# Who splits the first 64 key tiles, and one-hot arrays by fours of tokens

## The chip, the cores and the metric

The kernel runs on one core of a Trainium2 chip. The time is the device time of one launch in microseconds (us). TensorE is PE (its weight loads are PEld), VectorE is DVE, ScalarE is ACT, GpSimd is POOL, and SyncE is SP, which here only issues DMAs.

## The reference, cut to what matters

One decoder block on 256 tokens of width 1024: a mixer (conformer convolution and dilated attention), and then a layer of 16384 one-neuron experts, of which each token picks 16 in each of 8 heads:

```python
q = (xc @ w_q).reshape(TOKEN_CHUNK, PEER_HEADS, 2, half)
s = einsum('thpd,hpnd->thpn', q, sub_keys)            # 128 scores for each of 16 half keys
top_s, top_i = lax.top_k(s, PEER_TOPK)
cand = top_s[:, :, 0, :, None] + top_s[:, :, 1, None, :]
best_s, best_c = lax.top_k(cand.reshape(...), PEER_TOPK)
e = i1 * PEER_N_KEYS + i2                             # from top_i at best_c
gate = softmax(best_s)
h = einsum('thkd,td->thk', u_tab[e], xc)
act = gelu(h) * gate
y = einsum('thk,thkd->td', act, v_tab[e])
```

The kernel does not gather. It computes the gelu of all 16384 products with `u_tab`, multiplies each by its gate (zero for an expert that was not picked), and multiplies by all of `v_tab`.

## The kernel before, in words

All weights come in tiles of 128 x 1024 float32 (512 KB): 76 tiles `front` of the mixer and of `w_q`, 128 tiles of `u_tab` and 128 tiles of `v_tab`. They pass through one ring of four slots (RING). A tile in slot s goes through four engines:

- SP loads `raw[s]` when the lower part of the tile that held the slot before has been written (`load`, L348 to L351).
- ACT writes `hi[s]`, the tile rounded to the matmul's fast float32 format, once PE is done with the tile before in that slot (`split_hi`, L303 to L310).
- DVE or POOL writes `lo[s] = raw - hi` (`split_lo`, L319 to L324). `by_dve` (L312 to L314) says which of the two: DVE takes slot 3, and from tile G_SHARED = 143 on slot 1 too. Each of the two engines works through its instructions in the order in which they are written, so a split waits for what is written ahead of it.
- PE multiplies hi by hi, hi by the vector's low part and lo by hi: 24 matmuls of 256 columns a `u` tile (L1055), 12 of 512 columns a `v` tile (L1326).

ACT splits three tiles ahead of PE (LEAD = 3): while PE computes tile n, ACT writes `hi` of tile n + 3, and then the gelu of tile n (L573).

The expert layer has four stages. The first runs over the first 64 `u` tiles. In it, DVE works through 43 steps of the top-16 selection (`top_step`, L890; steps 0 to 15 are the first top 16, step 16 converts the indices, then for each of two chunks of 128 tokens one step that forms the candidates, L871, four of the second top 16, L857 to L862, one of small operations, L907 to L910, six that look the picked indices up, L881, L886 and L888 twice, and a last one, L916). A table `tile_of` spreads these steps over 48 of the 64 tiles, but only through the order of writing: nothing but the splits that stand among them (L934 to L941, one in four tiles) holds DVE back. Near the end PE transposes the picked indices and gates (L1297, L1301).

The second stage runs over the other 64 `u` tiles, the third over the first 64 `v` tiles. In both, every second tile, the gates of 8 tokens (TOK) are spread over 64 second keys: DVE makes `eqB` (L965), `ohA` (L967) and `ohB` (L971), float16 arrays of ones and zeros or gates, PE multiplies them token by token (L1283, 16 matmuls of 64 columns), and DVE multiplies the result into the gelu values (L983). In the third stage DVE also writes the low part of each vector, `nrm_lo` (L990). The fourth stage runs over the last 64 `v` tiles. The first u tiles up to tile 78 of all are split outside the stages' loops, by the same rule. POOL fills `iota_nk` (L409) between tile 78 and tile 79, the tile with which its loop over the 64 tiles of the change begins.

The one-hot arrays hold the tokens by pairs: in `ohA[:, g, q // PAIR, :, q % PAIR]` the 128 values of one token lie two elements (4 bytes) apart, and the two tokens of a pair alternate.

Of the kernel before, what the change touches and what calls it, by code (L numbers as in the profile page):

```python
# [10 lines left out]
F16 = mybir.dt.float16  # L11
ALU = mybir.AluOpType
# [3 lines left out]
P = 128  # L16
D = 1024
T = 256
# [10 lines left out]
PH, NK, TOPK = 8, 128, 16  # L29
# [14 lines left out]
LEAD = 3  # L44
# [6 lines left out]
WARM_UP = 12  # L51
G_SHARED = N_FRONT + HALF + LEAD
TOK = 8
PAIR = 2
GROUPS_N = T // TOK


# [79 lines left out]
    FREED[_job] = _n[freed_by_dve(_job)]  # L137


PAIRS = [(0, 2), (1, 3), (4, 6), (5, 7), (8, 10), (9, 11)]  # L140


C_N1, C_N2, C_GLU, C_DW, C_DWB = 0, 8, 16, 24, 24 + CB * TAPS
# [8 lines left out]
def hybrid_block(nc, x_t, front, cols, rel_bias, onehot, sub_keys, u_tiles, v_tiles, out):  # L152
    toeplitz = nc.dram_tensor("toeplitz", (HEADS, P * BW), F32, kind="Internal").ap()
    with ExitStack() as ctx:
        def sb(name, shape, dt=F32, stack=ctx):
            return stack.enter_context(nc.sbuf_tensor(name, shape, dt))
# [46 lines left out]
        resid = tmp("resid", [P, KB, T])  # L203
        inner.close()
        act = sb("act", [P, NK, T])
        iota_nk = sb("iota_nk", [P, NK, PAIR], F16)
        keys = sb("keys", [P, 2, T], F16)

        parts = sb("parts", [P, T // PAIR, 2, PAIR], F16)
        ohA = sb("ohA", [P, 2, TOK // PAIR, NK, PAIR], F16)  # L210
        eqB = sb("eqB", [P, 2, TOK // PAIR, HALF, PAIR], F16)
        ohB = sb("ohB", [P, 2, TOK // PAIR, 2, HALF, PAIR], F16)

        p3 = prob[:, :].rearrange("p (h n) -> p h n", n=BW)
        qT = prob[:, 0:HALVES * T].rearrange("p (u t) -> p u t", t=T)
# [79 lines left out]
        def slot_of(base, j):  # L295
            return (base + j) % RING
# [14 lines left out]

        def by_dve(base, j):  # L312

            return slot_of(base, j) == 3 or (base + j >= G_SHARED and slot_of(base, j) == 1)  # L314

        def wait_lo(eng, base, it, j):
# [65 lines left out]
        @block.gpsimd  # L382
        def _(pool):

            pool.memset(relx[BUCKETS:BUCKETS + 1, :], NEG).then_inc(const, 1)
            pool.wait_ge(const, 1)
            pool.memset(ones[:, :], 1.0).then_inc(const, 1)
            pool.memset(ident[:, :], 0.0).then_inc(const, 1)
            pool.memset(u_pad[:, :, 0:TAPS - 1], 0.0).then_inc(const, 1)
            pool.memset(kmask[:, :], 0.0).then_inc(const, 1)  # L390
            pool.wait_ge(const, 5)
            for r in range(2):
                pool.memset(kmask[r * HD:(r + 1) * HD, HEADS - 2 + r:HEADS - 1 + r], 1.0).then_inc(const, 1)
                pool.wait_ge(const, 6 + r)
            pool.affine_select(out=ident[:, :], in_=ident[:, :], compare_op=ALU.not_equal, fill=1.0,
                               base=0, pattern=[[-1, P]], channel_multiplier=1).then_inc(const, 1)
            pool.iota(iota[:, :], pattern=[[1, TOPK]], base=0, channel_multiplier=0,
                      allow_small_or_imprecise_dtypes=True).then_inc(const, 1)

            def lo_of(g):  # L400
                if not by_dve(g, 0):
                    split_lo(pool, g, 0, 0)

            for g in range(N_FRONT + LEAD):
                lo_of(g)

            pool.wait_ge(y_began, 1)
            pool.wait_ge(normed, 2 * KB)
            pool.iota(iota_nk[:, :, :], pattern=[[1, NK], [0, PAIR]], base=0, channel_multiplier=0,  # L409
                      allow_small_or_imprecise_dtypes=True).then_inc(const, 1)  # L410
            for base, tiles in ((U0 + LEAD, HALF), (G_SHARED, N_U + N_V - RING - HALF)):
                with pool.Fori(0, tiles // RING) as it:
                    for j in range(RING):
                        if not by_dve(base, j):
                            split_lo(pool, base, it, j)

        @block.scalar
        def _(a):
# [25 lines left out]
            split_hi(a, 2, 0, 0)  # L444

            def exp_of(s):
                c, pair = divmod(s, len(PAIRS))
                w = P * (c + 1)
                a.wait_ge(score_max, s + 1)
                for h in PAIRS[pair]:  # L450
                    pr = p3[:, h, c * P:c * P + w]
                    col = c * HEADS + h
                    a.activation(pr, pr, ACT.Exp, bias=negm[:, col:col + 1],
                                 accum_out=lsum[:, col:col + 1]).then_inc(exps, 1)
# [166 lines left out]
        def _(dve):  # L621
# [78 lines left out]

            def score(s):

                c, pair = divmod(s, len(PAIRS))
                h0 = PAIRS[pair][0]
                w = P * (c + 1)
                job_done(dve, ("score", s))
                for r, h in enumerate(PAIRS[pair]):
                    col = c * HEADS + h
                    ins = dve.scalar_tensor_tensor(out=p3[:, h, c * P:c * P + w],
                                                   in0=bank[BANK_OF[("score", s)]][:, r * w:(r + 1) * w],  # L710
                                                   scalar=rq[:, col:col + 1], in1=bias[:, h, T - w:T],
                                                   op0=ALU.mult, op1=ALU.add)
                    ins.then_inc(dve_evac if r else biased, 1)
                freed(dve, ("score", s))
                dve.wait_ge(biased, s + 1)
                dve.tensor_reduce(negm[:, c * HEADS + h0:c * HEADS + h0 + 3:2], p3[:, h0:h0 + 3:2, c * P:c * P + w],
                                  AX.X, ALU.max, negate=True).then_inc(score_max, 1)
# [214 lines left out]
            weights = [21] * HALVES + [10] + TC * ([23] + [35] * (PH // 2) + [8] + [23] * 6 + [3])  # L932
            tile_of = [int(TOP_TILES * sum(weights[:n]) / sum(weights)) for n in range(len(weights))]
            for i in range(HALF):  # L934
                if by_dve(U0 + LEAD, i):
                    split_lo(dve, U0 + LEAD, 0, i)
                for n, tile in enumerate(tile_of):
                    if tile == i:
                        top_step(n)
                if i == EXP_TILE + 2:  # L940
                    softmax_gates()  # L941
# [1 line left out]
            dve.tensor_copy(keys[:, :, :], bank[6][:, :].rearrange("p (a t) -> p a t", a=2)).then_inc(pick_ready, 1)  # L943
            dve.wait_ge(pick_T, 2)
            link(dve.tensor_scalar(pickf[:, 0, :], bank[7][:, 0:T], GATE_SCALE, None, ALU.mult))
            picked = pickf[:, 0, :].rearrange("p (a b) -> p a b", b=PAIR)
            link(dve.tensor_copy(parts[:, :, 0, :], picked))
            dve.tensor_tensor(parts[:, :, 1, :], picked, parts[:, :, 0, :], ALU.subtract).then_inc(pick_ready, 1)
            dve.wait_ge(pick_ready, 2)
# [2 lines left out]
            def one_hots(half, it, g):  # L952

                n = it * 2 + (half * GROUPS_N + g)
                t = bass.ds(it * (2 * TOK) + g * TOK, TOK)

                wait(dve, gate_mm, n - 1)

                def at(x, m):
                    return x.rearrange("p (a b) -> p a b", b=PAIR).unsqueeze(2).broadcast_to([P, TOK // PAIR, m, PAIR])  # L960

                def every_pair(x, m):
                    return x.unsqueeze(1).broadcast_to([P, TOK // PAIR, m, PAIR])

                dve.tensor_tensor(eqB[:, g % 2], every_pair(iota_nk[:, half * HALF:(half + 1) * HALF, :], HALF),  # L965
                                  at(keys[:, 1, t], HALF), ALU.is_equal).then_inc(second, 1)
                dve.tensor_tensor(ohA[:, g % 2], every_pair(iota_nk[:, :, :], NK), at(keys[:, 0, t], NK),  # L967
                                  ALU.is_equal).then_inc(spread, 1)
                dve.wait_ge(second, n + 1)
                two = bass.ds(it * (2 * TOK // PAIR) + g * (TOK // PAIR), TOK // PAIR)  # L970
                dve.tensor_tensor(  # L971
                    ohB[:, g % 2].rearrange("p a i n b -> p (a i) n b"),
                    eqB[:, g % 2].unsqueeze(2).broadcast_to([P, TOK // PAIR, 2, HALF, PAIR]),
                    parts[:, two, :, :].rearrange("p a i b -> p (a i) b").unsqueeze(2)
                    .broadcast_to([P, 2 * TOK // PAIR, HALF, PAIR]), ALU.mult).then_inc(spread, 1)

            def multiply(half, it, g):

# [56 lines left out]
        def _(pe):  # L1035
# [104 lines left out]
                step(ins)  # L1140

            def scores(s):
                c, pair = divmod(s, len(PAIRS))
                w = P * (c + 1)
                b = start(("score", s))
                freed(pe, ("kb", AB // 2 - 1))
                for r, h in enumerate(PAIRS[pair]):
                    rows = slice((h % 2) * HD, (h % 2 + 1) * HD)
                    ins = pe.matmul(b[:, r * w:(r + 1) * w], qk[rows, h // 2, c * P:(c + 1) * P],  # L1149
                                    qk[rows, AB + h // 2, 0:w], start=r == 0, stop=True, skip_group_check=True)  # L1150
                step(ins)
# [125 lines left out]
            def gates(half, it, g):  # L1277

                n = it * 2 + (half * GROUPS_N + g)
                pe.wait_ge(spread, n * 2 + 2)  # L1280
                for q in range(TOK):
                    for i in range(2):
                        ins = pe.matmul(bank[6 + g][:, q * HALF:(q + 1) * HALF], ohA[:, g, q // PAIR, :, q % PAIR],  # L1283
                                        ohB[:, g, q // PAIR, i, :, q % PAIR], start=i == 0, stop=i == 1, skip_group_check=True)
                ins.then_inc(gate_mm, 1)

            for j in range(RING):
# [131 lines left out]
```

## Time and profile before

| | us |
|---|---|
| median of 3 runs | 1069.43 |
| lowest, highest | 1066.47, 1072.64 |
| the profiled execution | 1069.04 |
| its span (first to last instruction) | 1067.3 |
| PE, DVE, ACT, POOL busy | 1049.8, 751.4, 509.7, 514.0 |

The mean granted TensorE clock of the profiled execution is 0.988 of full speed. The chain that ended last is 91% PE. By the trace the stages of the expert layer are: first stage about 298 to 491 us, second to 694, third to 886, fourth to 1063. A busy PE says little by itself, since matmuls are pipelined; what counts is how far their starts are apart, and the gaps. The duration of a DVE or POOL instruction in these rows includes time in which it had been issued and was held up, with no semaphore in play.

### The profile page before, as it was taken

How to read it: one execution, taken by the hardware profiler on the slowest of the kernel's cores; microseconds unless marked ns; L12 is line 12 of the kernel's file. 1: busy time of each engine (PE TensorE's matmuls, PEld its weight loads, DVE VectorE, ACT ScalarE, POOL GpSimd, SP SyncE). 2: the span in 40 equal slices, each digit the busy share in tenths (PEclk: the TensorE clock that was granted, in tenths of full speed). 3: DMA queues.
4: the chain of work that ended last, by engine and by line, in shares of the span. 5: the costliest groups of instructions: out<-in, count | busy, mean ns of one | idle time of the engine just before them, and what ended most of it. 6: DMA issues, size and time to landing. Idle time of an engine off the chain costs nothing.

```text
span 1067.3 us, 21882 instructions
## 1 busy us (share of the span) xinstructions
PE 1049.8 (98%) x7850; PEld 961.8 (90%) x7850; DVE 751.4 (70%) x1232; ACT 509.7 (48%) x798; POOL 514.0 (48%) x216
## 2 busy tenths in 40 slices
PE   8999999999999998999999999999999999999998
PEld 6999898999999998999999999978887777888886
DVE  5375868744079899918555555599999997777775
ACT  5453667545454443454444444444444444444553
POOL 3654452654646694964344333444434434444442
PEclk8999999999999998999999999999999999999999
DMA  5864342644535544465554455545554555666662
GB/s 195 267 209 139 125 149 84 216 160 141 182 133 183 191 148 166 140 214 174 167 172 158 161 173 168 166 158 177 177 172 162 177 177 178 197 196 188 190 194 97
DMA packets 52258, 181.91 MB, mean 170 GB/s; under 512 B 5851, under 2 KB 9051, under 8 KB 52092
## 3 DMA queue, kind: packets, MB, share of 16 engines
q1 hardware_dynamic: 52220, 181.41, 52.0%
q8 instruction: 24, 0.39, 0.1%
q14 instruction: 14, 0.11, 0.0%
HBM read 177.97 MB, written 3.41 MB: 170 GB/s over the span
## 4 chain that ended last, share of the span: by engine, by line
PE 91%; DVE 7%; issue 1%; ACT 1%; DMA 0%; SPq 0%; ACTq 0%; DVEq 0%
PE bank L1055 49%; PE bank L1326 33%; PE bank L1283 3%; PE bank L1136 2%; DVE lo L323 1%; PE bank L1065 1%; PE bank L1149 1%; PE bank L1263 1%; DVE gsig L829 1%; DVE prob L748 1%; DMA relx<-rel_bias 0%; DVE act L881 0%; DVE act L886 0%; DVE act L871 0%; PE bank L1243 0%
## 5 line engine op out<-in xcount | busy, mean ns | idle before, releaser
L323 POOL TENSOR_TENSOR lo<-raw,hi 128x1024 fp32r<-128x1024 f32 x202 | 511.1, 2535 | 538.5 <-ACT hi L310 538.1
L310 ACT CAST hi<-raw 128x1024 fp32r<-128x1024 f32 x332 | 347.9, 1048 | 200.9 <-PE bank L1326 189.8
L1055 PE MATMUL bank<-nrm_hi,hi 128*128 128x256 f32 x1504 | 433.4, 288 | 7.5 <-DVE lo L323 5.1
L1055 PE MATMUL bank<-nrm_lo,hi 128*128 128x256 f32 x1504 | 428.1, 285 | 0.0
L1055 PE MATMUL bank<-nrm_hi,lo 128*128 128x256 f32 x1504 | 427.9, 285 | 0.0
L1055 PEld LDWEIGHTS bank<-nrm_hi,hi 128*128 128x128 f32 x1504 | 291.1, 194 | 12.9 <-issue 7.7
L1055 PEld LDWEIGHTS bank<-nrm_lo,hi 128*128 128x128 f32 x1504 | 291.4, 194 | 0.1
L1055 PEld LDWEIGHTS bank<-nrm_hi,lo 128*128 128x128 f32 x1504 | 291.1, 194 | 0.0
L323 DVE TENSOR_TENSOR lo<-raw,hi 128x1024 fp32r<-128x1024 f32 x130 | 173.6, 1336 | 111.0 <-ACT hi L310 110.5
L990 DVE TENSOR_TENSOR nrm_lo<-act,nrm_hi 128x256 fp32r<-128x256 f32 x128 | 151.0, 1182 | 51.2 <-ACT nrm_hi L598 51.1
L1326 PE MATMUL bank<-hi,nrm_hi 128*128 128x512 f32 x512 | 160.6, 395 | 0.7 <-ACT nrm_hi L598 0.7
L1326 PE MATMUL bank<-hi,nrm_lo 128*128 128x512 f32 x512 | 158.9, 391 | 0.3 <-DVE nrm_lo L990 0.3
L1326 PE MATMUL bank<-lo,nrm_hi 128*128 128x512 f32 x512 | 158.0, 390 | 0.0
L573 ACT ACTIVATE act<-bank 128x256 f32 x128 | 49.1, 384 | 218.0 <-PE bank L1055 217.9
L1326 PEld LDWEIGHTS bank<-hi,nrm_lo 128*128 128x128 f32 x512 | 95.1, 188 | 22.9 <-DVE nrm_lo L990 3.7
L1326 PEld LDWEIGHTS bank<-lo,nrm_hi 128*128 128x128 f32 x512 | 96.1, 188 | 20.2
L1326 PEld LDWEIGHTS bank<-hi,nrm_hi 128*128 128x128 f32 x512 | 93.7, 188 | 18.7 <-issue 0.8
L983 DVE SCALAR_TENSOR_TENSOR act<-bank,act 128x512 f32 (+1 forms) x64 | 43.9, 685 | 83.6 <-PE bank L1283 83.6
L971 DVE TENSOR_TENSOR ohB<-eqB,parts 128x1024 f16<-128x1024 f16 x64 | 59.2, 925 | 0.0
L967 DVE TENSOR_TENSOR ohA<-iota_nk,keys 128x1024 f16<-128x1024 f16 x64 | 52.5, 820 | 0.0
L598 ACT CAST nrm_hi<-act 128x256 fp32r (+1 forms) x128 | 51.2, 402 | 0.1
L689 DVE SCALAR_TENSOR_TENSOR bank<-u_pad,prm,bank 128x256 f32<-128x256 f32 x116 | 46.7, 481 | 0.0
(172 smaller groups left out, 764.8 us busy)
## 6 DMA issues: line engine op xcount, KB each, us to landing
raw<-u_tiles SPq DMA_DIRECT2D x128, 512.0 KB, 3.4
raw<-v_tiles SPq DMA_DIRECT2D x128, 512.0 KB, 3.4
raw<-front SPq DMA_DIRECT2D x76, 512.0 KB, 3.4
toeplitz<-prob SPq DMA_DIRECT2D x12, 192.0 KB, 4.4
bias<-toeplitz SPq DMA_DIRECT2D x12, 128.0 KB, 4.1
resid<-x_t SPq DMA_DIRECT2D x2, 512.0 KB, 4.5
qk<-sub_keys SPq DMA_DIRECT2D x1, 1024.0 KB, 6.8
y<-act SPq DMA_DIRECT2D x2, 512.0 KB, 2.6
```

The source lines that it names most:

```text
L310: act_e.copy(hi[:, s, :], raw[:, s, :]).then_inc(hi_ready, 1)
L323: eng.tensor_tensor(lo[:, s, :], raw[:, s, :], hi[:, s, :].bitcast(F32), ALU.subtract)\
L573: a.activation(act[:, it * 4 + (base_i + j), :], bank[4 + j % 2][:, 0:T], ACT.Gelu).then_inc(gelu_done, 1)
L598: a.copy(nrm_hi[:, (base_i + j) % RING, :], act[:, it * 4 + (base_i + j), :]).then_inc(a_hi, 1)
L689: dve.scalar_tensor_tensor(out=acc[:, b, :] if w == TAPS - 1 else part_sum, in0=src, scalar=wt, in1=part_sum, op0=ALU.mult, op1=ALU.add).t ...
L967: dve.tensor_tensor(ohA[:, g % 2], every_pair(iota_nk[:, :, :], NK), at(keys[:, 0, t], NK), ALU.is_equal).then_inc(spread, 1)
L971: dve.tensor_tensor(ohB[:, g % 2].rearrange("p a i n b -> p (a i) n b"), eqB[:, g % 2].unsqueeze(2).broadcast_to([P, TOK // PAIR, 2, HALF, ...
L983: dve.scalar_tensor_tensor(out=av, in0=gv, scalar=1.0 / GATE_SCALE, in1=av, op0=ALU.mult, op1=ALU.mult)\
L990: dve.tensor_tensor(nrm_lo[:, s, :], act[:, it * 4 + (base_i + j), :], nrm_hi[:, s, :].bitcast(F32), ALU.subtract).then_inc(a_lo, 1)
L1055: ins = pe.matmul(dst, w_[:, s, u * P:(u + 1) * P], x_[:, k, :], start=first and i == 0 and p_ == 0, stop=last and i == n - 1 and p_ == 2)
L1283: ins = pe.matmul(bank[6 + g][:, q * HALF:(q + 1) * HALF], ohA[:, g, q // PAIR, :, q % PAIR], ohB[:, g, q // PAIR, i, :, q % PAIR], start= ...
L1326: ins = pe.matmul(bank[2 * c + half][:, :], a_[:, j, c * P:(c + 1) * P], v_[:, j, half * 512:(half + 1) * 512], start=False, stop=stop and ...
```

## The change

- `by_dve` returns False for the tiles 79 to 142 (from U0 + LEAD up to G_SHARED), whatever their slot. POOL's loop over these 64 tiles then splits all of them in place of three in four, and the 16 splits that stood among DVE's top-16 steps are gone. All other tiles are split as before.
- PAIR = 2 becomes QUAD = 4 in the layout of `iota_nk`, `parts`, `ohA`, `eqB` and `ohB`: the values of one token lie four elements (8 bytes) apart, and four tokens alternate. The element counts of the DVE instructions, and all matmuls, stay the same; the runs of adjacent elements with one broadcast value, which had two elements, have four. `iota_nk` has 512 elements a partition in place of 256.
- The views through which DVE writes and reads these arrays (`picked`, `at`, `every_pair`, `two` and the operands of L971) have the same replacement. The list PAIRS of attention heads is only renamed.

```diff
-PAIR = 2
+QUAD = 4
-        iota_nk = sb("iota_nk", [P, NK, PAIR], F16)
+        iota_nk = sb("iota_nk", [P, NK, QUAD], F16)
-        parts = sb("parts", [P, T // PAIR, 2, PAIR], F16)
-        ohA = sb("ohA", [P, 2, TOK // PAIR, NK, PAIR], F16)
-        eqB = sb("eqB", [P, 2, TOK // PAIR, HALF, PAIR], F16)
-        ohB = sb("ohB", [P, 2, TOK // PAIR, 2, HALF, PAIR], F16)
+        parts = sb("parts", [P, T // QUAD, 2, QUAD], F16)
+        ohA = sb("ohA", [P, 2, TOK // QUAD, NK, QUAD], F16)
+        eqB = sb("eqB", [P, 2, TOK // QUAD, HALF, QUAD], F16)
+        ohB = sb("ohB", [P, 2, TOK // QUAD, 2, HALF, QUAD], F16)
...
         def by_dve(base, j):
 
+            if U0 + LEAD <= base + j < G_SHARED:
+                return False
             return slot_of(base, j) == 3 or (base + j >= G_SHARED and slot_of(base, j) == 1)
...
-            pool.iota(iota_nk[:, :, :], pattern=[[1, NK], [0, PAIR]], base=0, channel_multiplier=0,
+            pool.iota(iota_nk[:, :, :], pattern=[[1, NK], [0, QUAD]], base=0, channel_multiplier=0,
...
             for i in range(HALF):
-                if by_dve(U0 + LEAD, i):
-                    split_lo(dve, U0 + LEAD, 0, i)
                 for n, tile in enumerate(tile_of):
                     if tile == i:
                         top_step(n)
...
-                        ins = pe.matmul(bank[6 + g][:, q * HALF:(q + 1) * HALF], ohA[:, g, q // PAIR, :, q % PAIR],
-                                        ohB[:, g, q // PAIR, i, :, q % PAIR], start=i == 0, stop=i == 1, skip_group_check=True)
+                        ins = pe.matmul(bank[6 + g][:, q * HALF:(q + 1) * HALF], ohA[:, g, q // QUAD, :, q % QUAD],
+                                        ohB[:, g, q // QUAD, i, :, q % QUAD], start=i == 0, stop=i == 1, skip_group_check=True)
```

## Rows read from the trace of the kernel before

**Rows 1.** The page, part 1: busy us, share of the span, instructions.
```profile
PE 1049.8 (98%) x7850; PEld 961.8 (90%) x7850; DVE 751.4 (70%) x1232; ACT 509.7 (48%) x798; POOL 514.0 (48%) x216
```

**Rows 2.** What PE waited for: us in total, times, longest; the largest of nine.
```profile
PE bank L1055 <- DVE lo L323: 5.1, 1, 5.1
```

**Rows 3.** The chain of waits from 290 to 500 us: start, us, what.
```profile
290.65 7.14 PE bank L1263 x64
297.79 80.71 PE bank L1055 x672
...
412.40 2.73 DVE lo L323
...
490.81 0.50 PE bank L1283 x16
```

**Rows 4.** Timeline of ACT: start, us, instruction, count, idle before and its releaser.
```profile
407.43 0.38 ACT L573 ACTIVATE act<-bank 128x256 f32 x1 [1.56 <-PE bank L1055]
407.71 1.04 ACT L310 CAST hi<-raw 128x1024 fp32r<-128x1024 f32 x1
410.31 0.38 ACT L573 ACTIVATE act<-bank 128x256 f32 x1 [1.55 <-PE bank L1055]
...
420.86 0.38 ACT L573 ACTIVATE act<-bank 128x256 f32 x1 [9.24 <-PE bank L1055]
...
426.96 0.39 ACT L573 ACTIVATE act<-bank 128x256 f32 x1 [1.56 <-PE bank L1055]
```

**Rows 5.** Stretches: us, PE busy, granted PE clock, DMA share, GB/s.
```profile
410.00:415.00 5.00, 0.17 (x2) 0.96 0.00 0
415.00:420.00 5.00, 4.74 (x22) 0.50 0.62 215
```

**Rows 6.** Timeline of POOL in the first stage: splits, alone and beside DVE.
```profile
365.63 2.40 POOL L323 TENSOR_TENSOR lo<-raw,hi 128x1024 fp32r<-128x1024 f32 x1 [0.48 <-ACT hi L310]
371.38 4.02 POOL L323 TENSOR_TENSOR lo<-raw,hi 128x1024 fp32r<-128x1024 f32 x1 [3.36 <-ACT hi L310]
375.37 4.45 POOL L323 TENSOR_TENSOR lo<-raw,hi 128x1024 fp32r<-128x1024 f32 x1
...
408.83 2.38 POOL L323 TENSOR_TENSOR lo<-raw,hi 128x1024 fp32r<-128x1024 f32 x1 [0.47 <-ACT hi L310]
```

**Rows 7.** Timeline of DVE in the same stretch.
```profile
370.85 2.29 DVE L881 TENSOR_TENSOR act<-act,iota 128x2048 f32<-128x2048 f32 x1
373.17 4.38 DVE L886 TENSOR_TENSOR act<-act 128x2048 f32<-128x2048 f32 x1
377.59 2.29 DVE L888 TENSOR_REDUCE act<-act 128x128 f32<-128x2048 f32 x1
...
394.45 3.47 DVE L323 TENSOR_TENSOR lo<-raw,hi 128x1024 fp32r<-128x1024 f32 x1
...
400.37 4.38 DVE L871 TENSOR_TENSOR act<-act 128x2048 f32<-128x2048 f32 x1
```

**Rows 8.** Groups of DVE instructions, 500 to 690 us: busy, mean ns, idle before.
```profile
L323 DVE TENSOR_TENSOR lo<-raw,hi 128x1024 fp32r<-128x1024 f32 x30 | 36.8, 1225 | 6.5 <-ACT hi L310 6.2
...
L967 DVE TENSOR_TENSOR ohA<-iota_nk,keys 128x1024 f16<-128x1024 f16 x30 | 20.6, 685 | 0.0
...
L965 DVE TENSOR_TENSOR eqB<-iota_nk,keys 128x512 f16<-128x512 f16 x30 | 12.6, 419 | 0.0
```

**Rows 9.** Timeline of DVE late in the third stage.
```profile
850.51 2.63 DVE L990 TENSOR_TENSOR nrm_lo<-act,nrm_hi 128x256 fp32r<-128x256 f32 x1
...
856.67 2.61 DVE L990 TENSOR_TENSOR nrm_lo<-act,nrm_hi 128x256 fp32r<-128x256 f32 x1
```

**Rows 10.** The chain of waits in the third stage: start, us, what.
```profile
730.41 0.50 PE bank L1283 x16
730.91 5.55 PE bank L1326 x24
```

**Rows 11.** Line 409: POOL's iota, duration ns min/median/max, first and last start.
```profile
L409 POOL IOTA iota_nk<- x1: 1504/1504/1504, 291.5 to 291.5; 128x256 f16 x1
```

More of the change, by code:

```diff
@@ L137 @@
     FREED[_job] = _n[freed_by_dve(_job)]
-PAIRS = [(0, 2), (1, 3), (4, 6), (5, 7), (8, 10), (9, 11)]
+QUADS = [(0, 2), (1, 3), (4, 6), (5, 7), (8, 10), (9, 11)]
 C_N1, C_N2, C_GLU, C_DW, C_DWB = 0, 8, 16, 24, 24 + CB * TAPS
@@ L446, in exp_of @@
             def exp_of(s):
-                c, pair = divmod(s, len(PAIRS))
+                c, pair = divmod(s, len(QUADS))
                 w = P * (c + 1)
                 a.wait_ge(score_max, s + 1)
-                for h in PAIRS[pair]:
+                for h in QUADS[pair]:
                     pr = p3[:, h, c * P:c * P + w]
@@ L701, in score @@
             def score(s):
-                c, pair = divmod(s, len(PAIRS))
-                h0 = PAIRS[pair][0]
+                c, pair = divmod(s, len(QUADS))
+                h0 = QUADS[pair][0]
                 w = P * (c + 1)
                 job_done(dve, ("score", s))
-                for r, h in enumerate(PAIRS[pair]):
+                for r, h in enumerate(QUADS[pair]):
                     col = c * HEADS + h
@@ L945, in _ @@
             link(dve.tensor_scalar(pickf[:, 0, :], bank[7][:, 0:T], GATE_SCALE, None, ALU.mult))
-            picked = pickf[:, 0, :].rearrange("p (a b) -> p a b", b=PAIR)
+            picked = pickf[:, 0, :].rearrange("p (a b) -> p a b", b=QUAD)
             link(dve.tensor_copy(parts[:, :, 0, :], picked))
@@ L959, in at @@
                 def at(x, m):
-                    return x.rearrange("p (a b) -> p a b", b=PAIR).unsqueeze(2).broadcast_to([P, TOK // PAIR, m, PAIR])
+                    return x.rearrange("p (a b) -> p a b", b=QUAD).unsqueeze(2).broadcast_to([P, TOK // QUAD, m, QUAD])
                 def every_pair(x, m):
-                    return x.unsqueeze(1).broadcast_to([P, TOK // PAIR, m, PAIR])
+                    return x.unsqueeze(1).broadcast_to([P, TOK // QUAD, m, QUAD])
                 dve.tensor_tensor(eqB[:, g % 2], every_pair(iota_nk[:, half * HALF:(half + 1) * HALF, :], HALF),
@@ L969, in one_hots @@
                 dve.wait_ge(second, n + 1)
-                two = bass.ds(it * (2 * TOK // PAIR) + g * (TOK // PAIR), TOK // PAIR)
+                two = bass.ds(it * (2 * TOK // QUAD) + g * (TOK // QUAD), TOK // QUAD)
                 dve.tensor_tensor(
                     ohB[:, g % 2].rearrange("p a i n b -> p (a i) n b"),
-                    eqB[:, g % 2].unsqueeze(2).broadcast_to([P, TOK // PAIR, 2, HALF, PAIR]),
+                    eqB[:, g % 2].unsqueeze(2).broadcast_to([P, TOK // QUAD, 2, HALF, QUAD]),
                     parts[:, two, :, :].rearrange("p a i b -> p (a i) b").unsqueeze(2)
-                    .broadcast_to([P, 2 * TOK // PAIR, HALF, PAIR]), ALU.mult).then_inc(spread, 1)
+                    .broadcast_to([P, 2 * TOK // QUAD, HALF, QUAD]), ALU.mult).then_inc(spread, 1)
             def multiply(half, it, g):
@@ L1142, in scores @@
             def scores(s):
-                c, pair = divmod(s, len(PAIRS))
+                c, pair = divmod(s, len(QUADS))
                 w = P * (c + 1)
@@ L1146, in scores @@
                 freed(pe, ("kb", AB // 2 - 1))
-                for r, h in enumerate(PAIRS[pair]):
+                for r, h in enumerate(QUADS[pair]):
                     rows = slice((h % 2) * HD, (h % 2 + 1) * HD)
```

## The prediction

> **What bounds the kernel now.** I read the busy times first, then what PE waited for, then the chain of waits, and last the timelines around the one long gap. PE is busy 98% of the span and DVE 70% [rows 1], so only what changes PE's pace or its gaps moves the time. PE waits long for an operand once: 5.1 us for a low part from DVE [rows 2], which is `by_dve`'s slot 3 among the top-16 steps. Otherwise the first stage is dense: 672 matmuls in 80.71 us are 28 tiles at 2.88 us [rows 3]. The gap has a second part. After it PE runs at granted clock 0.50 for a while, 1.2 in place of 2.4 GHz [rows 5]. The gelus on ACT follow PE's tiles and count the whole loss: from 410.31 to 426.96 there are three tiles, 16.65 us in place of 3 x 2.88 = 8.64, so the episode costs 8.0 us [rows 4].
>
> **Why DVE was late.** ACT had this tile's `hi` by about 403.1 (one of the splits three tiles ahead, 1.04 us each [rows 4]), but DVE came to the split at 412.40 [rows 3], after a candidate step that began at 400.37 [rows 7] and two pairs of second top-16 steps up to 412.40, 7.6 us.
>
> **The change, part by part.** *DVE's 16 splits go.* Alone such a split takes 1.2 us [rows 8]. DVE then has no wait left among its steps and runs through them ahead of the tiles; it had time to spare in this stage apart from the one late split, so what it saves is worth nothing but the end of that episode: -8.0 us, if POOL is on time. What DVE does next (the gates' operands) waits for PE's transposes at tile 60 and is not earlier in a way that PE sees.
>
> *POOL gets 16 more.* Alone it needs 2.40 us a tile [rows 6] against PE's 2.88, so it now keeps up with every tile with 0.48 to spare. How far may it fall behind? ACT casts from 407.71, POOL splits from 408.83 for 2.38 and is done at 411.21; the tile is for PE three tiles after the one that began at about 407.4, at 407.4 + 8.64 = 416.0 [rows 4, 6]. So the reserve is 4.8 us. Before, a POOL that was behind got a free tile in four; now it catches up by 0.48 a tile only.
>
> What makes it fall behind is in the durations. From 371.38 POOL's splits take 4.02 and 4.45 us, and DVE's L886 takes 4.38 where L881, of the same size, took 2.29 [rows 6, 7]. The ends explain it: L881 ends at 373.14 and POOL's split at 375.40, 2.3 us later; L886 ends at 377.55, 2.2 us after that; POOL's next one at 379.82, 2.3 us after that. The two engines take turns: a POOL split and a DVE instruction with two large SBUF inputs do not run together. L888, a reduction with one input, takes 2.29 with a split beside it [rows 7], so it takes no turn. Each long turn of DVE costs POOL 4.45 - 2.40 = 2.05 us.
>
> Debt of POOL, first burst: the lookups of chunk 0 are four long turns (L881, L886, twice), L916 is a short one, and the candidates of chunk 1 (L871) a fifth long one. I charge 5 x 2.05 + 0.2 = 10.5 us. It lasts 5 x 4.38 + 2 x 2.29 + 2.5 = 29 us, 10.1 tiles, which give back 10.1 x 0.48 = 4.8. Net 5.6 against a reserve of 4.8: PE stands 0.8 us. Followed turn by turn, as PE starts a tile only on the whole split, it is about 1.4. Then the second top 16 of chunk 1, four pairs in 2 x 7.6 us and 1.05 of small operations, is 5.6 tiles, 2.7 us back, so 2.1 of debt is left. Second burst: four long turns and a short one, 8.4 us, over 24.6 us, 8.5 tiles, 4.1 back: 6.4, over the reserve by 1.6; turn by turn about 2.6. Together 2.4 by the sums and 4.0 by turns; I take 4.0, as single pauses of 0.5 to 1.5 us. With POOL's own part of a turn 0.05 us shorter or longer the turns give 2.7 or 5.1. The clock stays at 2.4 GHz in my forecast: it fell behind a pause of 5.1 us [rows 2, 5], and these are shorter. First stage: -8.0 + 4.0 = -4.0.
>
> The candidates of chunk 0 come alone, one turn, and are hidden by the reserve. SP loads the next tile of a slot after `lo` is written: a late split delays the load by as much, but the cast that it feeds is itself wanted only after PE is through with the tile. At the reserve's end this closes to about nothing, and I cost it at 0; uncovered it would add some tenths of a us at each of five pauses, 1 us in all. Removing the slot-3 split from DVE at the very end of the stage also puts four splits in a row on POOL while DVE makes its first one-hots, whose turns are short (0.4 to 0.7 us alone [rows 8]): inside the reserve.
>
> *The iota* doubles to 512 elements: 1.5 us [rows 11] becomes at most 3.0, in a hole of POOL before the first tile of its loop: its end moves from 293.0 to about 294.5, and the split behind it starts after 300 us, with the cast of tile 79 behind the end of the scores at 297.79 [rows 3]. 0.
>
> *Fours on DVE.* `eqB` has 512 elements and takes 0.419, `ohA` 1024 and takes 0.685: 0.52 ns an element. The float32 split takes 1.225 for 1024 and L881 2.29 for 2048: 1.04 ns an element [rows 7, 8]. So pairs already run at twice the float32 rate, the fastest of any two-input row here, with the rest a fixed part that no layout touches. I take 0. Bounds: a quarter of the one-hots' time gained or lost, (0.419 + 2 x 0.685) / 4 = 0.45 us a group. In the second stage DVE waits much of the time, so that is hidden. In the third it is not: DVE's period of two tiles is 856.67 - 850.51 = 6.16 us late in the stage [rows 9], against PE's own 6.05, two `v` tiles in 5.55 and the gates' 0.50 [rows 10]. A gain is worth no more than the 0.1 us a group, some 2 us in all; a loss counts in full, 32 x 0.45 = 14 us.
>
> The Trainium skill, "VectorE: DVE Perf Modes", section "The perf-mode tier table", says that a two-input instruction on 16-bit data reaches two elements a cycle and no more. The rows' factor of two agrees, and by it the layout by fours gains nothing.
>
> *Fours on PE.* 1024 matmuls (64 groups of 16) read weights and columns with an 8-byte step in place of 4. Now a group takes 0.50 us, 31 ns a matmul [rows 3]. No row has an 8-byte step. Lower bound: 256 columns take 80.71 / 672 = 120 ns [rows 3], so 64 take 30 at the same rate, and there is 1 ns a matmul to gain, 1 us in all. Upper bound, by the nearest matmuls with 128 weights that are loaded at the float32 rate: 7.14 us for 64, 112 ns each [rows 3], so 1024 x 0.081 = 83 us. If only the column read halves, 1024 x 0.031 = 32 us. I take 0, nearest to the row of the same instruction at half the step.
>
> The Trainium skill, "SBUF — State Buffer", section "Door 1: The DMA port swizzle", speaks of 16-byte lines, with full bandwidth as long as two accesses in a row hit one line. An 8-byte step is just inside that, and by it the cost is 0; no row here shows it.
>
> **Sum.** 1069.04 for the profiled execution (span 1067.3 and 1.7 around it) - 4.0 = 1065.0. That execution stands 0.4 under the median 1069.43, so against the median I say 1065.4.
>
> **Rivals.**
> (A) POOL keeps up: the turns cost less than charged (DVE, now early, meets POOL's idle time), PE never stands. Gain 8.0: 1061.4. For it: each lone contended split is absorbed today. Against: two splits in a row already took 8.4 us for 5.8 us of PE [rows 6].
> (B) The pauses pull the clock down: two or three of them, up to 1.5 us each with one tile between, bring a stretch at 1.2 GHz like that of rows 5, which cost 8.0 - 5.1 = 2.9 us. One or two such: 1068 to 1071. For it: the drop after the one gap. Against: in such a stretch PE wants tiles more slowly, and POOL catches up.
> (C) The other side: PE's gate matmuls slow down with the 8-byte step, in the second and third stage, where PE sets the pace. It decides from 4.0 / 1024 = 4 ns a matmul on. At 62 ns: 1065.4 + 32 = 1097. A small form (35 to 40 ns) gives 1070 to 1075. Against it: pairs already have a step and show 31 ns.
> (D) The late split is not always that late. At 394.45 POOL had started its split just ahead of DVE's, and DVE's took 3.47 [rows 7]; had DVE been first, the chain up to 412.40 would be 2.3 us shorter, the gap some 2.8 us and perhaps without the clock's fall. If the runs of before differ in this (1066.47 to 1072.64), the gain shows as less: 1067.
>
> **How the numbers follow.** Forecast 0.47 (1062.5 to 1067.5), A 0.18, B 0.10, C 0.13, D 0.12. The middle 8 in 10 runs from 1060 (most of A inside) to 1073 (C's large form left out, about 0.10). What a measurement can tell from no change is 0.5%, 5.3 us: faster means under 1064.1. That is A, and a third of the forecast: 0.34. Slower, over 1074.8: C but its small form, 0.10, and some of DVE's bound: 0.12. The rest, 0.54, is within 0.5%.
>
> **What would show it.** In the first stage: no DVE row at L323; no wait of PE for DVE; DVE's last L916 about 25 to 30 us earlier than before; several waits of PE for POOL's L323 between 370 and 420 us, 3 to 5 us in all, none over 2; POOL's splits back to back there at 4.4 or 2.4 us. Clock 1.00 through that stretch. L965, L967, L971 at 0.42 and 0.69 in the second stage, and L1283 at 0.50 us a group; a group above 0.56 makes me wrong by C. No wait for POOL at all would be A, a clock of 0.50 in the stretch B.

## The result, and the profile after

| | before | changed |
|---|---|---|
| median, us | 1068.41 (6 runs) | 1094.19 (6 runs) |
| lowest, highest | 1066.47, 1072.64 | 1093.49, 1097.57 |
| profiled execution, its span | 1069.04, 1067.3 | 1093.61, 1091.8 |

The changed kernel is slower: ratio 1.0241, 95% interval 1.0216 to 1.0266. The forecast was 1065.4 with a range from 1060 to 1073. It is rival (C), in its large form, that came: PE's gate matmuls with an 8-byte step. In the changed kernel the lines of the first stages stand two lower than before: the split is L325, and L883, L888, L890 and L918 are what L881, L886, L888 and L916 were.

The chain of waits of the changed kernel (start, us, what), at the places that answer to [rows 3, 10] (a row at the end of a view's window shows only its part inside it):

```profile
290.03 7.14 PE bank L1263 x64
297.18 66.31 PE bank L1055 x552
...
424.92 49.19 PE bank L1055 x408
...
486.26 1.00 PE bank L1283 x16
487.27 5.80 PE bank L1055 x48
...
705.26 4.80 PE bank L1326 x20
...
731.59 5.54 PE bank L1326 x24
737.12 1.01 PE bank L1283 x16
...
912.09 2.42 DVE nrm_lo L990
914.55 15.48 PE bank L1326 x67
```

A group of gate matmuls takes 1.00 us where it took 0.50. The starts of the stages in this chain, beside those of the kernel before, give the balance. The kernel before has these starts (same view):

```profile
694.47 5.69 PE bank L1326 x24
...
889.98 10.04 PE bank L1326 x43
```

| stretch | before | changed | difference |
|---|---|---|---|
| up to the scores (L1263) | 290.65 | 290.03 | -0.6 |
| to the first gates | 200.16 | 196.23 | -3.9 |
| to the first `v` tile | 203.66 | 219.00 | +15.3 |
| to the 65th `v` tile | 195.51 | 209.29 | +13.8 |
| to the end of the span | 177.3 | 177.3 | 0 |

The sum is +24.5, which is 1091.8 - 1067.3. The stretch from the scores to the first gates gained what was forecast; the second and third stages lost over seven times that much in the one term that was set to 0.

What PE waited for in the changed kernel (us in total, times, longest), and its clock where the pauses are (us, PE busy, granted clock, DMA share, GB/s), against [rows 2, 5]:

```profile
PE bank L1055 <- POOL lo L325: 3.1, 4, 1.3
```

```profile
360.00:390.00 30.00, 28.41 (x235) 1.00 0.47 150
390.00:425.00 35.00, 33.45 (x278) 1.00 0.50 171
```

No wait for DVE's `lo` is left; four short ones for POOL's stand in its place, and the clock stays at 1.00, that is 2.4 GHz. POOL's timeline shows the turns (against [rows 6]): alone 2.40, then 4.07 and 4.46 where DVE's L883 and L888 had been issued before it. The one of 2.39 is the other half of a turn: DVE's next L883 is issued at 365.07 and takes 4.43, since it stands until POOL is done at 367.34. The reduction L890 (362.75, 2.29) runs beside the end of the 4.46 and is not held up.

```profile
353.49 2.40 POOL L325 TENSOR_TENSOR lo<-raw,hi 128x1024 fp32r<-128x1024 f32 x1 [0.48 <-ACT hi L310]
356.50 4.07 POOL L325 TENSOR_TENSOR lo<-raw,hi 128x1024 fp32r<-128x1024 f32 x1 [0.61 <-ACT hi L310]
360.53 4.46 POOL L325 TENSOR_TENSOR lo<-raw,hi 128x1024 fp32r<-128x1024 f32 x1
364.95 2.39 POOL L325 TENSOR_TENSOR lo<-raw,hi 128x1024 fp32r<-128x1024 f32 x1
367.31 4.45 POOL L325 TENSOR_TENSOR lo<-raw,hi 128x1024 fp32r<-128x1024 f32 x1
```

DVE's last step of the selection starts at 424.88 (before, at 448.43), which is 23.6 us earlier where 25 to 30 were forecast, and DVE then waits 26 us for the exp of the gates. Its one-hots of 500 to 690 us have the durations of [rows 8] (groups: busy, mean ns, idle before):

```profile
L967 DVE TENSOR_TENSOR ohA<-iota_nk,keys 128x1024 f16<-128x1024 f16 x28 | 19.2, 685 | 0.0
...
L965 DVE TENSOR_TENSOR eqB<-iota_nk,keys 128x512 f16<-128x512 f16 x28 | 11.7, 419 | 0.0
```

### The profile page after: what moved, and what is told of

It reads as the page before. It is cut to its first block, busy times and chain, and to the rows that moved or that the text cites. A ratio compares the mean times of both kernels' runs of the same rounds, so it can differ in the third digit from the quotient of the medians.

```text
span 1091.8 us, 21876 instructions
## 1 busy us (share of the span) xinstructions
PE 1076.1 (99%) x7850; PEld 991.1 (91%) x7850; DVE 731.1 (67%) x1216; ACT 509.6 (47%) x798; POOL 546.2 (50%) x232
## 4 chain that ended last, share of the span: by engine, by line
PE 88%; DVE 4%; issue 4%; POOL 3%; ACT 1%; DMA 0%; SPq 0%; POOLq 0%; ACTq 0%; DVEq 0%
PE bank L1055 45%; PE bank L1326 32%; PE bank L1283 6%; POOL lo L325 3%; PE bank L1136 2%; PE bank L1149 1%; PE bank L1263 1%; DVE gsig L831 1%; DVE prob L750 1%; DMA relx<-rel_bias 0%; PE bank L1196 0%; PE bank L1065 0%; DVE rs L643 0%; PE bank L1243 0%; DVE gsig L828 0%
## 5 line engine op out<-in xcount | busy, mean ns | idle before, releaser
L325 POOL TENSOR_TENSOR lo<-raw,hi 128x1024 fp32r<-128x1024 f32 x218 | 543.6, 2503 | 530.9 <-ACT hi L310 530.6
L990 DVE TENSOR_TENSOR nrm_lo<-act,nrm_hi 128x256 fp32r<-128x256 f32 x128 | 170.9, 1337 | 68.3 <-ACT nrm_hi L600 68.3
L325 DVE TENSOR_TENSOR lo<-raw,hi 128x1024 fp32r<-128x1024 f32 x114 | 144.0, 1263 | 57.7 <-ACT hi L310 57.6
L1283 PE MATMUL bank<-ohB,ohA 128*128 128x64 f16 x1024 | 74.5, 242 | 0.0
L1283 PEld LDWEIGHTS bank<-ohB,ohA 128*128 128x128 f16 x1024 | 63.1, 118 | 9.5 <-issue 8.1
L971 DVE TENSOR_TENSOR ohB<-eqB,parts 128x1024 f16<-128x1024 f16 x64 | 48.2, 753 | 0.0
```

Source lines behind the costliest of these rows:

```text
L325: eng.tensor_tensor(lo[:, s, :], raw[:, s, :], hi[:, s, :].bitcast(F32), ALU.subtract)\
L971: dve.tensor_tensor(ohB[:, g % 2].rearrange("p a i n b -> p (a i) n b"), eqB[:, g % 2].unsqueeze(2).broadcast_to([P, TOK // QUAD, 2, HALF, ...
L990: dve.tensor_tensor(nrm_lo[:, s, :], act[:, it * 4 + (base_i + j), :], nrm_hi[:, s, :].bitcast(F32), ALU.subtract).then_inc(a_lo, 1)
```

## The experiments

All are variants of the changed kernel unless said otherwise, and their line numbers are up to six higher. The time of before is measured beside each set.

### 1. Only the splits, and only the layout

The first run puts the layout back to pairs (`QUAD = 2`). The second takes the kernel before and changes only the layout:

```diff
-PAIR = 2
+QUAD = 4
         def by_dve(base, j):
             return slot_of(base, j) == 3 or (base + j >= G_SHARED and slot_of(base, j) == 1)
```

> The changed kernel with the layout back at pairs: POOL splits all of the tiles 79 to 142, nothing else differs from the kernel before. Theory (the turns of POOL and DVE on the first stage, the 8-byte step the whole of the loss): gates at 0.50 us a group again, PE's second stage begins about 4.5 us earlier than before (486.3 in the changed kernel's trace against 490.8), pauses of PE for POOL of 3 to 4 us in all, and a time of 1064 +- 2 us. Rival (the first stage gains nothing in the time, since the profiled executions of before differ in their late split): 1067 to 1069. Rival (part of the loss comes from POOL's extra splits, in the later stages): over 1072.

> The kernel before with only the layout changed to fours; DVE keeps its 16 splits. Theory (8-byte step): 1.00 us a group of gate matmuls in place of 0.50, 64 groups, 32 us, less the up to 3 us by which the third stage was waiting for DVE anyway: 1068.4 + 29 to 32 = 1097 to 1100 us, and slower than the changed kernel by the 4 us of the first stage. Rival (the loss needs both parts): near 1068 or near 1094.

| | median, us | ratio to before (1070.09) |
|---|---|---|
| pairs, POOL splits all 64 | 1065.04 | 0.9958 (0.9944 to 0.9973) |
| fours, DVE keeps 16 splits | 1101.5 | 1.0283 (1.0258 to 1.0307) |

The splits alone gain 5.0 us by the medians, 2.9 to 6.0 by the interval (forecast 4.0, against the profiled execution). The layout alone costs 31 us, near the 32 of 64 groups. In the first of the two the gates take 0.50 us again and start at 485.41, and PE waits for POOL as in the changed kernel:

```profile
PE bank L1055 <- POOL lo L325: 3.2, 4, 1.3
```

In the second PE waits for DVE twice, 7.7 us in all with 5.1 the longest, which is more than in the profiled execution of before [rows 2]. So the changed kernel is the sum of two parts, and the chains of waits show it stretch by stretch:

| from the start of | to the start of | before | changed | pairs, POOL splits | fours, DVE keeps 16 |
|---|---|---|---|---|---|
| the scores | the first gates | 200.16 | 196.23 | 196.26 | 201.93 |
| the first gates | the first `v` tile | 203.66 | 219.00 | 203.66 | 219.00 |
| the first `v` tile | the 65th | 195.51 | 209.29 | 195.48 | 209.29 |

By these rows the layout costs 29.1 us, whoever splits, and the splits gain 3.9. The run with fours alone was expected at 1097 to 1100 us, 4 slower than the changed kernel; it is 1101.5 and 7 slower. In the first row its second late split shows as 1.8 us over before. The scores, ahead of all that the edits touch, start anywhere from 288.99 to 292.39 us in the twelve traces here, so that a single execution is uncertain by 3 us before the first stage begins.

### 2. Weights or moving columns

The arrays get layouts of their own, QA for `ohA` (weights) and QB for `eqB`, `parts` and `ohB` (moving columns):

```diff
-                        ins = pe.matmul(..., ohA[:, g, q // QUAD, :, q % QUAD],
-                                        ohB[:, g, q // QUAD, i, :, q % QUAD], ...)
+                        ins = pe.matmul(..., ohA[:, g, q // QA, :, q % QA],
+                                        ohB[:, g, q // QB, i, :, q % QB], ...)
```

> The changed kernel with ohA (the 128 weight columns) by fours and eqB, parts and ohB (the 64 moving columns) by pairs. If the weight load is what an 8-byte step slows: 1.00 us a group and about 1094 us. If the moving columns are: 0.50 us a group and about 1064. If each operand carries a part: between, 1075 to 1085. In the changed trace a weight load shows 118 ns against 97 and a matmul 242 against 193, which says nothing on which of them is first.

> The mirror of the run with the weights by fours: ohA by pairs, eqB, parts and ohB by fours. If the weight load is what the 8-byte step slows: 0.50 us a group, about 1064 us. If the moving columns are: 1.00 us, about 1094.

> ohA (weights) by eights, a 16-byte step, eqB, parts and ohB by pairs; POOL splits all 64. So far a group takes 0.50 us with both at 4 bytes, 0.55 with the weights at 8, 0.98 with the moving columns at 8 and 1.99 with both at 16. If weights are fetched by as many bytes as they span, their load (0.55 at 8 bytes) comes to about 1.0 us a group at 16 and the time to 1090; if they are fetched in parts side by side, 0.6 and 1067.

### 3. A 16-byte step, and no step

The fifth run has `QUAD = 8`. In the sixth PE reads adjacent elements of the same arrays, written by fours, so its gates are not the reference's:

```diff
+ohA[:, g, :, :, :].rearrange("p a n b -> p (a n b)")[:, q * NK:(q + 1) * NK]
+ohB[:, g, :, :, :, :].rearrange("p a i n b -> p (a i n b)")[:, (2 * q + i) * HALF:(2 * q + i + 1) * HALF]
```

> The changed kernel with the tokens by eights: a 16-byte step for weights and moving columns. The runs so far: 0.50 us a group at 4 bytes, 0.98 with the moving columns at 8 (0.55 with the weights at 8). If at 8 bytes each moving column is already fetched by itself, 16 bytes cost no more: 1.0 us a group, 1093 us. If the rate falls with the bytes stepped over: 2.0 us a group, 64 more us, 1155. By a rule of 16-byte lines that wants two columns in one line (the Trainium skill, SBUF — State Buffer, Door 1: The DMA port swizzle), the cliff would lie between 8 and 16 bytes, and 8 would have been free, which it was not.

> The changed kernel, in which PE reads the same one-hot arrays as runs of adjacent elements (128 weights, 64 columns) in place of one token's elements: the gates come out wrong, the time is what counts. If adjacent columns are no faster than a 4-byte step: 0.50 us a group and 1064 us. If the 4-byte step costs something too: below 0.50, at most 0.25 us a group and 1050.

The results of both sets, with a group of 16 gate matmuls as the chain of waits has it between 590 and 610 us (POOL splits all 64 tiles in each row):

| weights' step | columns' step | group, us | median, us | ratio to before |
|---|---|---|---|---|
| 2 bytes | 2 bytes | 0.48 | 1063.50 | 0.9940 (0.9920 to 0.9959) |
| 4 | 4 | 0.50 | 1065.04 | 0.9958 (0.9944 to 0.9973) |
| 8 | 4 | 0.55 | 1068.88 | 0.9986 (0.9969 to 1.0003) |
| 4 | 8 | 0.98 | 1092.44 | 1.0215 (1.0197 to 1.0232) |
| 8 | 8 | 1.00 | 1094.19 | 1.0241 (1.0216 to 1.0266) |
| 16 | 4 | 1.00 | 1094.03 | 1.0231 (1.0191 to 1.0271) |
| 16 | 16 | 1.99 | 1154.66 | 1.0784 (1.0752 to 1.0816) |

The ratios are each to the before of its own set: 1068.41 for the changed kernel, 1070.09 for the runs with 4/4, 8/4 and 4/8 bytes, 1069.27 for the first and last rows, 1069.12 for 16/4.

The rows of the chain behind five of them: adjacent, weights by fours, columns by fours, weights by eights, both by eights.

```profile
593.12 0.48 PE bank L1283 x16
```

```profile
590.70 0.55 PE bank L1284 x16
```

```profile
595.50 0.98 PE bank L1284 x16
596.48 5.79 PE bank L1056 x48
```

```profile
594.49 1.00 PE bank L1284 x16
595.49 5.82 PE bank L1056 x48
```

```profile
596.94 1.99 PE bank L1283 x16
598.92 5.75 PE bank L1055 x48
```

What follows: it is the moving columns that an 8-byte step slows. A matmul of 64 columns takes 30 ns with adjacent columns, 31 at a 4-byte step and 61 at 8. With columns and weights at 16 it takes 124. From 4 bytes on this is the time of the bytes passed over: 256, 512 and 1024 bytes in 31, 61 and 124 ns, 8.3 bytes a ns. The float32 matmuls fit it, 256 adjacent columns of 4 bytes in 120 ns [rows 3]: 8.5. Below 4 bytes a column nothing is gained: 64 adjacent float16 columns in 30 ns are 0.47 ns a column, and so are the float32 ones. The 4-byte step of pairs was thus the last tried that is free. The weights show the same one step later: at 8 bytes nearly free (0.55), at 16 a group takes 1.00. The point at 16 bytes is the least sure, since no run has the columns at 16 alone. If the two operands don't add up, the columns have the whole 124 ns. If the 31 ns that the weights at 16 add beside columns at 4 came on top here too, the columns would have 93. That a column costs the same at 16 bytes as at 8 is out either way: that gives 62 or 92. Against a sum is that the weights at 8 bytes add 0.05 us a group beside columns at 4 and 0.02 beside columns at 8.

The rule of the Trainium skill that the prediction named ("SBUF — State Buffer", section "Door 1: The DMA port swizzle": 16-byte lines, two accesses in one line for full bandwidth) would make an 8-byte step free for the columns. The runs show half the rate: 0.98 us a group against 0.50.

The second expectation, at most 0.25 us for adjacent columns, is out: 0.48.

### 4. What makes POOL late

The four multiplies of the lookups (L886, L888 in the changed kernel) are left out, with pairs and POOL splitting all 64:

```diff
                 elif stage == 1:
+                    return
```

> Pairs, POOL splits all 64, and the four multiplies L886 of the lookups left out, so the picked indices are wrong: 4 of the 9 long turns of DVE are gone. Theory (turns cost POOL 2 us each): POOL's debt is 4.1 us lower after each burst, inside its reserve of 4.8, and the 3.2 us of pauses for POOL vanish: 1061 to 1062. Rival (POOL's pace of 2.4 us against 2.88 is too tight by itself): pauses stay.

1061.83 us, ratio 0.9927 (0.9902 to 0.9953) against 1069.27. PE has no wait for a `lo` any more; what is left in the list is of other stages, 1.8 us the largest. That is 3.2 us less than the 1065.04 of the run with the multiplies, in another set of runs, whose before was 0.8 lower; the intervals of the two ratios just overlap. The trace is clearer than the times: from the scores to the first gates it is 192.16 us, against 196.26 with the multiplies. The picked indices are wrong in this run. DVE had 26 us to spare in this stage, so it is the turns of the multiplies that held PE up, and not the time that they take on DVE.

### 5. Two versions to beat both

The seventh run gives DVE four splits back, beside the lookups, with pairs and POOL's loop over the 64 tiles written out:

```diff
+DVE_TILES = (24, 28, 40, 44)
             for i in range(HALF):
+                if i in DVE_TILES:
+                    split_lo(dve, U0 + LEAD, 0, i)
```

> Pairs, and DVE splits 4 of the 64 tiles (the 25th, 29th, 41st and 45th of them, slot 3, beside the lookups), POOL the other 60. Theory (POOL's debt during the two bursts of lookups is what is left): each DVE split spares POOL one of 2.4 us where its debt is highest, and holds DVE back to PE's pace; no pause of PE in the first stage, 3 to 4 us less than with POOL alone, 1061 to 1062 us. Rival (a split on DVE comes late again, as in the kernel before): a pause for DVE of 1 to 5 us, 1063 to 1068.

1064.07 us, ratio 0.9938 (0.9916 to 0.9960). The rival came, a late split of DVE again, at the last of the four. The chain of waits:

```profile
424.29 4.39 DVE act L892
...
431.03 3.34 DVE lo L326
...
434.51 5.56 PE bank L1061 x32
```

PE waited 2.5 us for it, and behind that pause its clock fell to half for some 3 us (the window from 435 us: 0.66):

```profile
435.00:440.00 5.00, 5.00 (x31) 0.66 0.79 254
```

A pause of 2.6 us in the run with fours alone, the one that ends at 455.90, had no such stretch (the window from 455 us: 1.00):

```profile
455.00:460.00 5.00, 4.09 (x34) 1.00 0.60 201
```

What sets the two apart is open. The ninth leaves all splits to POOL, with pairs, and paces DVE instead:

```diff
-EXP_TILE = 52
+EXP_TILE = 56
+PACE = {26: 32, 29: 37, 36: 47, 39: 53}
...
                     if tile == i:
+                        if n in PACE:
+                            dve.wait_ge(hi_ready, U0 + PACE[n] + 1)
                         top_step(n)
```

> Pairs, POOL splits all 64 tiles, and DVE, which in the changed kernel runs ahead of the tiles, waits at four of its steps until ACT has cast a given tile: the second lookup of chunk 0 for tile 32 of the stage, L916 for 37, the first and second lookup of chunk 1 for 47 and 53. The exp of the gates moves from tile 52 to 56, so that nothing waits for the later end of DVE. Theory (POOL's debt comes from long turns that follow each other; it gains back 0.48 us a tile in between): no pause of PE for POOL above 0.3 us in the first stage, 3 us less than with POOL alone (1065.0), 1061 to 1063 us. Rival (the pauses have another cause, as POOL's queue or the loads): pauses of 3 us stay and the time is 1064 to 1066.

1061.72 us (7 runs, 1059.90 to 1063.41), ratio 0.9927 (0.9899 to 0.9954) against 1069.12. By its median it is the fastest version here that computes the block; its interval overlaps those of the run with pairs and of the one before. PE's one wait for POOL in the first stage (us, times, longest), and two windows of it (us, PE busy, granted clock, DMA share, GB/s), in which PE has no gap:

```profile
PE bank L1058 <- POOL lo L326: 0.2, 1, 0.2
```

```profile
300.00:350.00 50.00, 50.00 (x419) 1.00 0.51 169
350.00:400.00 50.00, 50.00 (x419) 1.00 0.52 172
```

The length from the scores to the first gates ranks the versions better than their times do, as it leaves out what differs ahead of the scores:

| | us | over the shortest |
|---|---|---|
| fours, DVE keeps 16 splits | 201.93 | 9.8 |
| before | 200.16 | 8.0 |
| pairs, four splits on DVE | 196.34 | 4.2 |
| pairs, POOL splits all | 196.26 | 4.1 |
| changed | 196.23 | 4.1 |
| pairs, POOL splits all, DVE paced | 192.55 | 0.4 |
| pairs, no multiplies | 192.16 | 0 |

The last one has no wait of PE in this stage. The 8.0 of before and the 4.1 of POOL's turns are the two terms of the prediction.

## Why the prediction was wrong

**The step that failed** is "Fours on PE ... I take 0, nearest to the row of the same instruction at half the step". The row at half the step was at the last free step, and said nothing of the next one. It measured +0.50 us a group: 1.00 against 0.50, on 64 groups, 29.1 us in the two stages. The bound "if only the column read halves, 1024 x 0.031 = 32 us" was the right size; rival (C) had 0.13 of the chance and its large form lay outside the range. Two things in the text could have warned. The matmuls of pairs were shown at 31 ns against 30 of the column rate, so that there was no reserve on PE, and any slowing counted in full. And float32 columns, 4 bytes each, run at that same rate, so no row showed PE taking more than 4 bytes of each partition a column: a read that passes over 8 was outside of what the trace covered, and wanted a run of its own or a larger chance.

**Where C's price was off.** 1065.4 + 32 = 1097 was given and 1094.2 measured. The second stage lost 15.3 and the third 13.8 us, and not 16 each (32 groups of 0.50). In the second a pair of tiles with its gates takes 6.80 us where it took 6.33, since the tiles got 0.03 shorter. In the third PE had been held back late in the stage by DVE's period of 6.16 us [rows 9]; with 1.01 + 5.54 = 6.55 a pair of tiles PE is the slower one, and the tenth of a us a group that it waited before is inside the new time.

**DVE's late split**, -8.0 us: right. The wait for DVE is gone and no stretch at half clock is left in that stage; before's stage is 8.0 us longer than the one without pauses.

**POOL's debt**, +4.0 us in pauses of 0.5 to 1.5: right in its sum. The list has 3.1 us in four waits, of 1.3, 0.3, 0.2 and 1.3, so two are shorter than forecast; the stage as a whole is 4.1 us longer than without pauses. The sum of the stage, -4.0, was measured as -3.9 between the scores and the first gates, and as 5.0 us in the time by the run with pairs. That the turns are the cause is shown by the run without the multiplies and by the paced one.

**Rival (A)**, no pauses: not so. **Rival (B)**, the clock: not so, 1.00 in both windows with pauses. But the reason given against it, that the clock fell behind a pause of 5.1 us and these are shorter, had less room than it seemed: in the run with four splits on DVE it fell behind one of 2.5. **Rival (D)**, that before's episode is often smaller: not borne out; its gain of 2.4 us lies just outside the 2.9 to 6.0 of the run with pairs against 17 runs of before. The run with fours alone has the first stage of before, and its trace shows the same episode: a late split at 414.01 and a wait of 5.1 us. How often it comes stays open with two traces.

**Fours on DVE**, 0: right, 685 and 419 ns as before. **The iota**: right that it is hidden; the bound of 3.0 us held, but it got shorter and not longer, see below.

## What to carry to other kernels

Before changing a layout, work out how many bytes each reader passes over per element, for the engine that is the bound first of all: what a writer is indifferent to can halve the rate of the reader. A row at one step does not price the next step; where the reader runs exactly at its rate, a larger step is a risk that wants its own run. An engine with enough time on average can still be late where another one takes turns with it: look for its instructions that take longer than their like, charge each turn, and pace the other engine where it has time to spare, here 26 us.

## What the runs showed of the hardware that was not expected

- Moving columns: 31 and 61 ns for 64 float16 columns at 4 and 8 bytes apart, and 124 at 16 with the weights at 16 too. Weights: 128 of them at 8 bytes cost 0.05 us more in a group of 16, at 16 bytes 0.50.
- POOL's iota of 512 elements is shorter than that of 256: 1181 ns against 1504 [rows 11]. The other traces agree: 1.50 to 1.51 us for 256 elements, 1.18 to 1.19 for 512, and 1.61 for 1024. Why is open.

```profile
L411 POOL IOTA iota_nk<- x1: 1181/1181/1181, 290.9 to 290.9; 128x512 f16 x1
```

- DVE's small one-input copies wait for a turn as well, which the prediction did not charge. In the timeline of DVE in the run with pairs, a copy of 128 elements takes 2.33 us, issued just behind the start of a split of POOL's (401.01, 2.40), and the next one 0.23, between two splits, while a reduction over 2048 elements keeps its 2.29:

```profile
401.17 2.33 DVE L911 CAST act<-act 128x128 f32<-128x128 uint32 x1
403.53 0.23 DVE L912 CAST act<-act 128x128 f32<-128x128 uint32 x1
...
410.53 2.29 DVE L890 TENSOR_REDUCE act<-act 128x128 f32<-128x2048 f32 x1
```
